# Which place of a 13-row ring a gather takes: rotation replaced by the expected order of release

## What is computed

```python
def peer(h, w_q, sub_keys, expert_u, expert_v):      # h: the RMS-normed tokens, D = 1024
    t = h.reshape(T, D)
    q = (t @ w_q).reshape(T, 8, 2, 64)
    s = einsum('thpd,hpnd->thpn', q, sub_keys)        # 8 heads, 2 halves, 128 keys
    ts, ti = top_k(s, 16)
    cand_s, cand_i = ...                              # 16 x 16 sums, numbers of 16384 experts
    best_s, best_j = top_k(cand_s, 16)
    ids, gates = ..., softmax(best_s)                 # 8 x 16 = 128 experts a token
    act = gelu(einsum('td,thkd->thk', t, expert_u[ids]))
    return einsum('thk,thkd->td', gates * act, expert_v[ids])
```

## Time and profile before

| | us |
|---|---|
| median of three runs | 3514.77 |
| the three runs | 3514.76, 3514.77, 3531.49 |
| span of the profiled execution | 3513.9 |
| POOL: gathers, busy in all | 2134.5 of the span |
| first gather issued, last gather issued | 104.1, 3498.1 |

### The profile page before, as it was taken

How to read it: one execution, slowest core, us unless ns; L and a number is a source line. 1 busy time by engine, 2 the same in 40 slices (tenths; PEclk the granted TensorE clock), 3 DMA queues, 4 the chain that set the end, 5 groups by cost and what they waited for, 6 DMA issues and landing times.

```text
span 3513.9 us, 25147 instructions
## 1 busy us (share of the span) xinstructions
PE 2235.1 (64%) x7990; PEld 803.6 (23%) x7990; DVE 2176.4 (62%) x5644; ACT 259.6 (7%) x506; POOL 2135.6 (61%) x2184
## 2 busy tenths in 40 slices
PE   7123866466765774577868366757787754555487
PEld 6112213121311141123213122412321311100011
DVE  3988288776656776635467876783626777655500
ACT  3000100100000000001100100000010000000000
POOL 0365566656665655666566656566756665666665
PEclk9655888787987867799989687668899877877699
DMA  6587898999898989997897999899789889899998
GB/s 236 221 334 287 297 367 308 393 342 368 321 381 343 361 328 411 410 409 270 314 371 289 384 336 375 311 368 374 300 303 355 329 337 356 339 386 385 372 381 324
DMA packets 331598, 1201.44 MB, mean 342 GB/s; under 512 B 40898, under 2 KB 41290, under 8 KB 329418
## 3 DMA queue, kind: packets, MB, share of 16 engines
q0 software_dynamic: 313344, 1140.99, 85.7%
q1 hardware_dynamic: 17034, 49.94, 3.8%
q10 hardware_dynamic: 1088, 8.91, 0.6%
HBM read 1188.82 MB, written 10.87 MB: 341 GB/s over the span
## 4 chain that ended last, share of the span: by engine, by line
POOL 25%; another core or an unknown queue 17%; issue 17%; DVE 17%; PE 16%; DMA 6%; ACT 2%; ACTq 0%; POOLq 0%; DVEq 0%
POOL rows L590 25%; PE acc L975 6%; DVE rows L1422 6%; DMA rows<-in_expert_v,idsT 4%; PE psA L807 4%; PE psB L917 2%; DVE work L1151 1%; PE psA L798 1%; PE psB L834 1%; DMA rows<-in_expert_u,ids 1%; DVE work L1230 1%; DVE work L1237 1%; DVE work L1227 1%; DVE work L1271 1%
## 5 line engine op out<-in xcount | busy, mean ns | idle before, releaser
L975 PE MATMUL acc<-rows,strip 128*32 128x512 f32 x4352 | 1414.0, 667 | 672.6 <-DMA rows<-in_expert_v,idsT 486.5
L1422 DVE CUSTOM_DVE_ANT_0 rows<-rows,psH 128x1024 f32<-128x1024 f32 x1088 | 1291.8, 1218 | 402.8 <-DMA rows<-in_expert_u,ids 247.4
L590 POOL DMA_INDIRECT rows<-in_expert_v,idsT x1088 | 1106.8, 1017 | 690.3 <-issue 297.8
L590 POOL DMA_INDIRECT rows<-in_expert_u,ids x1088 | 1027.7, 945 | 672.5 <-issue 316.2
L975 PEld LDWEIGHTS acc<-rows,strip 128*32 128x32 f32 x4352 | 268.8, 116 | 1697.6 <-issue 853.1
L807 PE MATMUL psA<-hT,w_in_sb 128*128 128x128 f32 (+1 forms) x1280 | 203.7, 314 | 105.3 <-issue 105.0
L807 PEld LDWEIGHTS psA<-hT,w_in_sb 128*128 128x128 f32 x1280 | 189.4, 230 | 134.6 <-issue 134.6
L1151 DVE SCALAR_TENSOR_TENSOR work<-zbuf,chan,work 128x128 f32<-128x128 f32 (+1 forms) x870 | 215.3, 324 | 5.8 <-DVE work L1151 3.8
L798 PE MATMUL psA<-w_out_sb,hT 128*128 128x512 f32 x320 | 160.4, 644 | 17.8 <-ACTq L661 9.2
L917 PE MATMUL psB<-w_q_sb,hT 128*128 128x512 f32 x288 | 140.7, 638 | 39.0 <-issue 15.4
L1429 DVE TENSOR_TENSOR x_out<-acc,x_out 128x1024 f32<-128x1024 f32 (+1 forms) x10 | 12.2, 1220 | 244.6 <-PE acc L975 207.5
(11 more groups left out here) (181 smaller groups left out, 1289.2 us busy)
## 6 DMA issues: line engine op xcount, KB each, us to landing
rows<-in_expert_u,ids POOLq DMA_INDIRECT x1088
rows<-in_expert_v,idsT POOLq DMA_INDIRECT x1088
w_in_sb<-in_w_in ACTq DMA_DIRECT2D x4, 2176.0 KB
w_in_sb<-in_w_in SPq DMA_DIRECT2D x4, 2176.0 KB
w_out_sb<-in_w_out SPq DMA_DIRECT2D x2, 4096.0 KB
w_q_sb<-in_w_q SPq DMA_DIRECT2D x2, 4096.0 KB
x_out<-x_mid SPq DMA_DIRECT2D x10, 512.0 KB
x_mid<-x_mix SPq DMA_DIRECT2D x8, 512.0 KB
```

The source lines that it names most:

```text
L590: nc.gpsimd.indirect_dma_start(out=rows[:, j, :], out_offset=None, in_=table[:, :], in_offset=bass.IndirectOffsetOnAxis(ap=index, axis=0))\
L975: last = nc.tensor.matmul(acc[LS * a:LS * (a + 1), half:half + 512], strip[:, first:first + LS], rows[:, at % RING, half:half + 512], star ...
L1422: nc.vector.tensor_tensor_reduce(rows[:, j, :], rows[:, j, :], psH[:, :], 1.0, 0.0, ALU.mult, ALU.add, dots[:, r:r + 1]).then_inc(s_free[j ...
```

## The change

The list of gathers, their order and what consumes them stay as they are. What changes is which of the 13 places a gather takes. A small loop at build time keeps for each place the number at which its row is counted as used: for u the gather's own number, for v its number plus `V_STAYS = 3`. Each gather takes the place with the lowest such number. A place that holds a row of v is so taken again up to three gathers later than by rotation, and one with a row of u up to three earlier. Every wait and count on `s_free` and `s_row` goes by `PLACE` and by `TURN_OF`, the number of times that the place was taken before.

```diff
+V_STAYS = 3
-    AT = {key: i for i, key in enumerate(FETCHES)}
+    PLACE, TURN_OF, ends, turns = {}, {}, list(range(-RING, 0)), [0] * RING
+    for at, key in enumerate(FETCHES):
+        j = ends.index(min(ends))
+        PLACE[key], TURN_OF[key] = j, turns[j]
+        ends[j] = at + (V_STAYS if key[0] == "v" else 0)
+        turns[j] += 1
     def landed(engine, key):
-        engine.wait_ge(s_row[AT[key] % RING], 16 * (AT[key] // RING + 1))
+        engine.wait_ge(s_row[PLACE[key]], 16 * (TURN_OF[key] + 1))
     def done(engine, key):
-        engine.wait_ge(s_free[AT[key] % RING], AT[key] // RING + 1)
+        engine.wait_ge(s_free[PLACE[key]], TURN_OF[key] + 1)
...
-            for at, (kind, m, i) in enumerate(FETCHES):
-                j = at % RING
+            for kind, m, i in FETCHES:
+                j, turn = PLACE[kind, m, i], TURN_OF[kind, m, i]
...
-                if at == RING - 1:
+                if j == RING - 1 and turn == 0:
                     pool.wait_ge(s_sc2, 1)
-                if at >= RING:
-                    pool.wait_ge(s_free[j], at // RING)
+                if turn:
+                    pool.wait_ge(s_free[j], turn)
```

More of the change, by code:

```diff
@@ L163, in build @@
     FETCHES = [key for n in range(ITEMS + 1) for tick in range(TICKS) for key in merged(u_at(n, tick), v_at(n, tick))]
-    AT = {key: i for i, key in enumerate(FETCHES)}
-    assert len(AT) == sum(picks(v) + width(v) for v in range(ITEMS))
+    assert len(set(FETCHES)) == sum(picks(v) + width(v) for v in range(ITEMS))
+    PLACE, TURN_OF, ends, turns = {}, {}, list(range(-RING, 0)), [0] * RING
[4 more added lines that the diff above has]
+        turns[j] += 1
     def landed(engine, key):
-        engine.wait_ge(s_row[AT[key] % RING], 16 * (AT[key] // RING + 1))
+        engine.wait_ge(s_row[PLACE[key]], 16 * (TURN_OF[key] + 1))
     def done(engine, key):
-        engine.wait_ge(s_free[AT[key] % RING], AT[key] // RING + 1)
+        engine.wait_ge(s_free[PLACE[key]], TURN_OF[key] + 1)
     def last_u(n):
@@ L964, in add_tokens @@
                     for _, v, i in some:
-                        at = AT["v", v, i]
+                        j = PLACE["v", v, i]
                         k = GROUPS.index((v, i // GROUP))
@@ L975, in add_tokens @@
                         last = nc.tensor.matmul(acc[LS * a:LS * (a + 1), half:half + 512], strip[:, first:first + LS],
-                                                rows[:, at % RING, half:half + 512], start=b == 0, stop=b == LS - 1,
+                                                rows[:, j, half:half + 512], start=b == 0, stop=b == LS - 1,
                                                 skip_group_check=True)
                         if half:
-                            last.then_inc(s_free[at % RING], 1)
+                            last.then_inc(s_free[j], 1)
             def first_projection():
@@ L1417, in take_row @@
             def take_row(n, r):
-                j = AT["u", n, r] % RING
+                j = PLACE["u", n, r]
                 if r == 0:
```

## The result

| | us |
|---|---|
| kernel before, median of 4 runs | 3518.17 (3514.76 to 3531.49) |
| changed kernel, median of 4 runs | 3550.82 (3539.85 to 3554.62) |
| ratio, with its 95% interval | 1.0076 (1.0046 to 1.0105) |
| span of the profiled execution, before and after | 3513.9, 3548.3 |

The change makes the kernel 0.76% slower by the ratio, which is 27 us; the two medians lie 33 us apart. The forecast of 3508 us was wrong, and the time lies above the range, which ended at 3533.

The account below looks back on a forecast made before the run. POOL's closed stream of gathers was taken as the bound, with the DMA engines behind it. -17 us (v's longer stays) and +10 us (u's shorter) made -7 us against 3513.9, a time of 3508 us; range 3455 to 3533 us.

Parts of the forecast that it names:

- POOL's stream closes: First to last gather: gathers, gaps without waiting and 646.5 us of waits for a place fill POOL's whole 3395 us.
- the DMA engines are full outside the taps: Outside ticks 8 to 13: DMA share 0.98 or more, 1.40 us a gather, so less waiting only lengthens the queue.
- Longer stays in the taps: Ticks 8 to 13, items 1 to 8 (eight stretches): 13 gathers earlier, 17 us won, bounds 0 and 31.
- I take zero here: Price of v's longer stays outside ticks 8 to 13, since the DMA engines are full around such waits.
- Longer stays elsewhere: 46 more waits on rows of v, 134 us, outside ticks 8 to 13: zero gain, bounds 0 and 94 us.
- Rival A: Late signals don't depend on the queue, so waits on v elsewhere are saved: 55 us more, 3453 us; chance 0.27.
- Shorter stays for u: Four item starts and a wait in item 2's tick 20: 8 gathers, 10 us lost, bounds 0 and 57.
- Rival B: Ticks 0 to 25: places of u become the wait, "DVE dots" rises by 40 or more; 3555 us; chance 0.13.
- the half case: Half of the slower rival's cost, where rows of u become what POOL waits for: 3535 us.
- Rival C: Gathers issued early are caught in DVE's tap runs and the lead is lost: +7 us, 3522 us; chance 0.12.
- the milder half of B: The less slow outcomes of u becoming the wait, which the range up to 3533 us took in.
- The bound of 57 us for the u side: Most that u's shorter stays could cost: twenty gathers waiting longer if every release came as in the trace.

Follow-up runs that it names:

- e6: Kernel before, rotation kept, plus a wait for the same row of u ahead of the 509 gathers that the change lets take u's place early; 1.0029 (1.0000 to 1.0058).
- e17: Kernel before with the change's rule for every row of v but those gathered in ticks 7 to 13, where places rotate; 1.0070 (1.0043 to 1.0098).
- e18: Kernel before with the change's rule only for rows of v gathered in ticks 7 to 25, without the starts of items; 1.0012 (0.9989 to 1.0034).
- e5: The changed kernel run again, unaltered, against the kernel before; 1.0070 (1.0043 to 1.0096).
- e9: Kernel before, where each gather also waits until the gather six before it has landed; 1.0009 (0.9984 to 1.0035).

## Why the prediction was wrong, point by point

- **That POOL's stream closes** held: its parts account for 34.1 of the 34.4 us.
- **That the DMA engines are full outside the taps** was read from three stretches of 0.98 and more. Taken by stages over the turns of items 1 to 9, the share outside ticks 8 to 13 is 0.87 to 1.03, and 0.94 to 0.99 in ticks 0 to 7. They are nearly full, and "I take zero here" leant on more than that.
- **Longer stays in the taps.** The stops moved by the predicted numbers of gathers, and the rule in these ticks alone brings 9 us where 17 were reckoned (0 to 31). The term had the right sign, at half its size. A later stop is also a longer one when PE's date is fixed (10.67 for 8.71 us), and DVE's late row is only the next one. In the whole change nothing of it is seen: 1.0070 without the rule in the taps, 1.0070 and 1.0076 with it.
- **Longer stays elsewhere at zero, and below zero only by way of the u side: this step failed.** With the early waits for u in place (e6), the longer stays of v cost 13 us (4 to 22) more, where -17 and zero stood in the sum. Outside the taps the rule costs 25 us (e17, 1.0070), and without the starts of items nothing that can be told (e18). The prediction had the mechanism in hand, "three more gathers in the queue would then let the signal come later", and put it at nothing. The traces show such a signal, ahead of ACT's copy in tick 7, later by 18 to 26 us in all wherever the rule of three holds at every start. How much of the loss goes by it stays open.
- **Rival A** falls. At tick 17 the signal did not keep its time when POOL ran on, but came 24.9 us after its matmul instead of 22.0. "remote" fell by 17 us, not by 50, and in the repeat it is 308.7 us, above the 296.2 of before.
- **Shorter stays for u** stood at 8 gathers, 10 us, and the early waits alone cost 10 us (0 to 21, e6). The size was right, the way to it was partly luck. It listed the waits for u that the trace of before had, four item starts and one more. In the changed kernel POOL waits longest at others, as in tick 7 of item 3 for 8.94 us, and "DVE dots" is 87 us with the early waits alone and 120 to 123 with both sides. The two sides were priced apart, against the same trace, and then added; they are one after the other in one stream.
- **Rival B, with 0.13 too low,** is what happened, by the mark given to it: "DVE dots" up by 49.6 us, where 40 were asked for. Its price, 40 us for the full and 20 for the half case, fits the 27 to 33 us, but by luck in part: its mechanism, a shorter lead over DVE, is what e6 has alone, and that costs 10 us. The rest came with v's longer stays, and some of the new waits on DVE are DVE's own wait behind a late signal. What spoke against B, that DVE had only 73.7 us of POOL's waits, was no argument: it told how often DVE was last with 13 gathers of lead, not with 12 or 10. Over the 16 kernels and repeats, ratio and "DVE dots" go together (correlation 0.82, 0.11 points for 10 us).
- **Rival C** falls. The gathers' time over 0.94 us, added up over the eight stretches, is 74.8 us before and 70.0 in the changed kernel, so no more is caught there than was. Single gathers are still caught beside the taps (one of 5.47 us below), as the Trainium skill (SBUF — State Buffer, "Who interferes with whom") has it; what the rival would make of that rule for the lead as a whole isn't seen.

```profile
2840.28 3.95 POOL L597 DMA_INDIRECT rows<-in_expert_v,idsT  x1 [2.81 <-PE acc L982]
...
2847.03 5.47 POOL L597 DMA_INDIRECT rows<-in_expert_u,ids  x1 [0.30 <-issue]
```

The first of these rows is item 8's stop of the earlier trace rows, one gather later, as predicted, and 2.81 us for 2.11.

- **The range** took in only the milder half of B. The bound of 57 us for the u side, which was on paper, would have carried it to 3572 with nothing won in the taps.

## What to carry to other kernels

When a buffer place that frees late gets more time, some other place gets less; with a fixed ring the lead is only moved from one consumer to another, and the consumer that has little waiting now may have it because of that lead. Price both sides in one walk through the stream, with the new order of places and each release at the time of its consumer, not each from the waits of the old trace. Such a walk has its limit: with every duration fixed it could not have charged the change more than the early waits for u alone, which cost 10 us here. So ask as well which steps came late behind the stream in the old trace, and what they do when the stream runs further ahead, and give that a price of its own even if it is a guess. And if the price is some tenths of a per cent, test the rule by region with many runs: a stage of two single traces pointed at the wrong place here.

## What the hardware showed beside that

Signals between engines came late while gathers were in the queue. ACT's square root follows a matmul of PE. In the nine turns after the first, from the timelines, it started over 18 us after the matmul's end three times in the kernel before (20.7, 22.0 and 18.9 us) and three times in the changed one (19.5, 24.9 and 19.2); each of the six came 5.2 to 6.7 us after the last gather was issued, while POOL stood. In the repeat of the change (e5) one signal of 18.7 us came 1.2 us after a gather's issue, and in e9 one of 19.1 us 1.9 us after, so that a long stop is not the only way. With at most three gathers on their way at an issue there was no such case, all nine started within 0.05 us, but the DMA engines then ran at 320 GB/s for 380. With at most five nothing was won. ACT's copy in tick 7 does the same (the table above). Whether the signal itself is late or ACT is not ready to take it, and whether that passes through what the gathers keep busy, these runs do not tell.
